# x in two halves, operand splits moved into the projections they follow, and output blocks between the last MLA scores

## The reference, cut to what matters

```python
def mla_layer(x, pos, norm_g, w_in, q_norm_g, w_q_up, kv_norm_g, w_kv_up, q_gain, k_gain, w_out):
    z = rms_norm(x, norm_g) @ w_in
    cq, ckv, k_pe, gate = jnp.split(z, [...], axis=-1)          # 512, 512, 64, 2048 wide
    q = (rms_norm(cq, q_norm_g) @ w_q_up).reshape(b, s, A_HEADS, A_QK)
    kv = (rms_norm(ckv, kv_norm_g) @ w_kv_up).reshape(b, s, A_HEADS, A_NOPE + A_V)
    ...
    o = mla_attend(q, k, v, pos).reshape(b, s, A_WIDTH)         # masked softmax(q k) v
    return x + (o * jax.nn.silu(gate)) @ w_out

def diff_layer(x, pos, layer_idx, norm_g, w_in, q_gain, k_gain, lq1, lk1, lq2, lk2, subln_g, w_out):
    z = rms_norm(x, norm_g) @ w_in                              # q, k, v, gate: each 2048 wide
    ...
    o = diff_attend(q, k, v, pos, lam)                          # softmax - lam * softmax, times v
    o = rms_norm(o, subln_g) * (1.0 - lam_init)
    return x + (o.reshape(b, s, B_WIDTH) * jax.nn.silu(gate)) @ w_out
```

## Time and profile before

| | us |
|---|---|
| median of 3 runs | 3446.47 |
| lowest, highest | 3445.31, 3449.75 |
| the profiled execution | 3445.53 |
| its span in the profile | 3443.7 |
| PE busy | 3324.7 (97%) |
| DVE busy | 1534.2 (45%) |
| POOL busy | 2101.6 (61%) |
| ACT busy | 707.8 (21%) |
| mean granted clock | 0.982 of 2.4 GHz |

### The profile page before, as it was taken

The page is one execution under the profiler, slowest core; times in us unless marked ns, Lnnn a source line. Parts: engine busy times, 40 slices in busy tenths (PEclk is TensorE's granted clock), DMA queues, the critical chain, the costliest instruction groups (busy, mean ns, idle before and its releaser), DMA issues.

```text
span 3443.7 us, 63823 instructions
## 1 busy us (share of the span) xinstructions
PE 3324.7 (97%) x21442; PEld 2648.1 (77%) x21442; DVE 1534.2 (45%) x3108; ACT 707.8 (21%) x1284; POOL 2101.6 (61%) x3492
## 2 busy tenths in 40 slices
PE   8999999998999989899989998999999999999899
PEld 6777777777787877678867777787888888788687
DVE  3444444445666763571246666213433243323500
ACT  2111111102323220130024444101211111111200
POOL 6444444445767748688764433787666666766566
PEclk9999999999999989899999999999999999999999
DMA  4111111112222213223321111232222222222232
GB/s 152 51 50 45 50 50 50 44 50 68 71 75 67 73 49 92 76 79 92 92 63 39 39 37 37 83 95 83 74 79 79 73 73 73 80 74 78 61 104 79
DMA packets 459579, 239.42 MB, mean 70 GB/s; under 512 B 27901, under 2 KB 456120, under 8 KB 458936
## 3 DMA queue, kind: packets, MB, share of 16 engines
q1 hardware_dynamic: 455656, 232.19, 23.1%
q10 hardware_dynamic: 3792, 5.28, 0.4%
HBM read 233.22 MB, written 4.19 MB: 69 GB/s over the span
## 4 chain that ended last, share of the span: by engine, by line
PE 85%; DVE 6%; issue 4%; POOL 2%; ACT 1%; SPq 1%; DVEq 0%; DMA 0%; ACTq 0%; POOLq 0%; PEldq 0%
PE proj L321 23%; PE proj L322 21%; PE proj L323 21%; POOL w_lo L311 2%; PE work L2293 2%; PE work L1114 1%; PE work L656 1%; PE work L670 1%; PE work L1926 1%; PE work L664 1%; PE work L630 1%; PE work L321 1%; PE work L639 1%; PE work L323 1%; PE work L322 1%
## 5 line engine op out<-in xcount | busy, mean ns | idle before, releaser
L307 POOL TENSOR_SCALAR w_hi<-raw_weights 128x256 fp32r<-128x256 f32 x1744 | 745.3, 455 | 1326.3 <-PE proj L323 1310.6
L311 POOL TENSOR_TENSOR w_lo<-raw_weights,w_hi 128x256 fp32r<-128x256 f32 x1744 | 1372.5, 818 | 0.0
L321 PE MATMUL proj<-x_hi,w_hi 128*128 128x512 f32 x2976 | 1234.1, 415 | 40.5 <-POOL w_lo L311 14.1
L322 PE MATMUL proj<-x_lo,w_hi 128*128 128x512 f32 x2976 | 1183.3, 398 | 0.0
L323 PE MATMUL proj<-x_hi,w_lo 128*128 128x512 f32 x2976 | 1182.8, 397 | 0.0
L321 PEld LDWEIGHTS proj<-x_hi,w_hi 128*128 128x128 f32 x2976 | 563.6, 189 | 205.5 <-issue 48.5
L323 PEld LDWEIGHTS proj<-x_hi,w_lo 128*128 128x128 f32 x2976 | 563.0, 189 | 138.0
L322 PEld LDWEIGHTS proj<-x_lo,w_hi 128*128 128x128 f32 x2976 | 565.1, 190 | 117.0 <-issue 2.2
L321 PE MATMUL proj<-o_hi,w_hi 128*128 128x512 f32 x256 | 103.5, 404 | 7.3 <-POOL w_lo L311 3.6
L321 PE MATMUL proj<-lat_hi,w_hi 128*128 128x512 f32 x224 | 97.5, 435 | 8.6 <-DVE lat_lo L1733 4.0
L322 PE MATMUL proj<-o_lo,w_hi 128*128 128x512 f32 x256 | 102.1, 399 | 0.0
(11 more groups left out here) (465 smaller groups left out, 4251.4 us busy)
## 6 DMA issues: line engine op xcount, KB each, us to landing
raw_weights<-w_in SPq DMA_DIRECT2D x260, 256.0 KB, 3.2
raw_weights<-b_w_in SPq DMA_DIRECT2D x256, 256.0 KB, 3.1
raw_weights<-a_w_in SPq DMA_DIRECT2D x100, 256.0 KB, 3.2
raw_weights<-w_out SPq DMA_DIRECT2D x64, 256.0 KB, 2.9
raw_weights<-a_w_out SPq DMA_DIRECT2D x64, 256.0 KB, 3.0
raw_weights<-b_w_out SPq DMA_DIRECT2D x64, 256.0 KB, 2.9
raw_weights<-a_w_kv_up SPq DMA_DIRECT2D x32, 256.0 KB, 2.8
mix<-x SPq DMA_DIRECT2D x4, 1024.0 KB, 8.2
```

The source lines that it names most:

```text
L307: pool.tensor_scalar(part(hi_v, s % 2, q), part(raw_v, s, q), 1.0, 1.0, ALU.mult, ALU.mult).then_inc(hi_done, 1)
L311: pool.tensor_tensor(part(lo_v, s % 2, q), part(raw_v, s, q), part(hi_v, s % 2, q).bitcast(F32), ALU.subtract).then_inc(w_split, 1)
L321: pe.matmul(out, w_h, a_h, start=start, stop=False)
L322: pe.matmul(out, w_h, a_l, start=False, stop=False)
```

## The change

Eight edits, in the order of the program.

1. `x_hi` and `x_lo` become two buffers each, for blocks 0 to 7 and 8 to 15, laid out hi0, lo0, hi1, lo1. `xh` and `xl` are now lists of blocks. PSUM banks are numbered anew (`j % 4`, `LAT_BANK`, `MLA_BANK`).
2. At the ends of LAT, MLA and OUT2 a new `stage_left` takes the place of most `stage_end` calls: it counts and does not wait.
3. LAT: the four q latents are split during the last latent tile; the sums of the kv latents stand in MLA behind 4 blocks; each kv split follows the norm of its block.
4. MLA's last pair: OUT2's first-half blocks stand where other pairs have projection blocks, four ahead of the first scores, one in each step, two in each of the last two. Operand blocks 0 to 3 are split ahead of the first scores, 4 to 7 one in each of steps 4 to 7, 8 to 15 behind the pair.
5. OUT2's last group: blocks 0 to 7 of DIFF's operand are split between its additions, once its first halves are done; blocks 8 to 15 behind it.
6. DIFF: the sums of squares stand behind its first tile, and the reciprocal root follows them.
7. DIFF's last head: the eight OUT3 splits stand ahead of the last gate (`before_scores()` moves up one line), and ACT starts them when half of the last tile is projected.
8. OUT1's loop over groups is unrolled.

```diff
+        x_parts = [[fixed.take(f"x_{part}{g}", UNIT_KB * SEQ, F32R) for part in ("hi", "lo")] for g in range(2)]
...
+        def stage_left(eng, own):
+
+            for s, value in own:
+                eng.wait_ge(s, value)
+            eng.sem_inc(stage_done, 1)
...
+                if k == 2 * LB - 2:
+                    tile_done(act, U_LAT + 4 * LB - 2)
+                    latent_high(act, range(LB))
...
             for k in range(LB, 2 * LB):
-                scaled(lat[:, k], U_LAT + 2 * k + 1, proj[BANK(T_LAT, k)])
+                if k == 2 * LB - 1:
+                    for b in range(LB):
+                        latent_low(dve, b)
+                scaled(lat[:, k], U_LAT + 2 * k + 1, proj[LAT_BANK(k)])
...
             pe.wait_ge(LN2_DVE.sem, LN2_DVE.done(f"lo{LB - 1}"))
-            run(part, 5)
+            run(part, LB)
+            sums_of_latent(pe, 1)
+            run(part, LB)
             kv_rstd_pe(pe)
-            run(part, 7)
-            pe.wait_ge(LN2_DVE.sem, LN2_DVE.done(f"lo{2 * LB - 1}"))
-            run(part, 8)
+            run(part, LB)
+            for k in range(LB, 2 * LB):
+                pe.wait_ge(LN2_DVE.sem, LN2_DVE.done(f"lo{k}"))
+                run(part, 1)
+            run(part, LB)
...
+            for parts in mla_heads_pe(pe, A_HEADS // 2 - 1, 4, ()):
+                run(part, parts)
+            run(part)
+            stage_left(pe, [])
...
+            two = [out_half(pe, OUT2, 0, j, 0) for j in range(2)]
+            for part in two * 2:
+                for _ in range(UNIT_KB // 2):
+                    next(part)
+                    yield
+            for j in (2, 3):
+                yield from out_half(pe, OUT2, 0, j, 0)
...
+                    if k >= TB:
+                        split(range(k, k + 1))
...
+                if TB <= k < HB:
+                    split(range(k, k + 1))
...
+            for j, before, between in ((0, range(0, 4), ()), (1, range(4, 6), ()), (2, range(6, 8), ()), (3, (), range(8, 9))):
+                norm_b_low(dve, before)
+                add_tile(dve, OUT2, KB // 4 - 1, j)
+                norm_b_low(dve, between)
+                add_squares(KB - 4 + j)
+            norm_b_low(dve, range(9, KB))
...
             def split_first():
-                act.wait_ge(w_used, SPLIT_SLOTS + U_OUT3)
+                tile_done(act, U_OUT3 - 2)
                 out_split_act(act, OUT3, FIRST)
...
+            before_scores()
             gate_tanh_of(1)
-            before_scores()
...
+            before_scores()
             take_gate(1)
-            before_scores()
```

More of the change, by code:

```diff
@@ L244, in build @@
         lo_v = w_lo[:, :].rearrange("p (s k c) -> p s k c", s=SPLIT_SLOTS, k=UNIT_KB)
-        xh = tokens(x_hi[:, :], SEQ)
-        xl = tokens(x_lo[:, :], SEQ)
+        xh, xl = ([tokens(x_parts[b // UNIT_KB][part][:, :], SEQ)[:, b % UNIT_KB] for b in range(KB)]
+                  for part in range(2))
         mix_v = tokens(mix[:, :], SEQ)
@@ L1037, in build @@
         o_lo4 = tokens(nc.alloc_sbuf_tensor_at("o_lo4", [P, KB * SEQ], F32R, offset=o_start)[:, :], SEQ)
-        OUT1 = OutStage("out1", 4, U_OUT1, T_OUT1, mix_v, o_hi4, o_lo4)
+        OUT1 = OutStage("out1", 4, U_OUT1, T_OUT1, mix_v, *([v[:, b] for b in range(KB)] for v in (o_hi4, o_lo4)))
         OUT1.o_hi_at = stage_start
@@ L1413, in add_tile @@
                 dve.tensor_tensor(acc_q[:, :], acc_q[:, :], q4[:, :], ALU.add).then_inc(d_summed, 1)
-            for j in range(4):
-                add_tile(0, j)
-            with dve.Fori(1, KB // 4) as i:
+            for i in range(KB // 4):
                 for j in range(4):
@@ L2026, in mla_heads_dve @@
             done(dve.tensor_tensor(m_qr[:, :], m_qr[:, :], m_tmp[:, :], ALU.add), "qrr")
+            split(range(0, 4))
             need(MA_PE, "sums")
@@ L2096, in build, with add_tile @@
         h_all_summed = sem("h_all_summed")
[L2098 to L2109 removed]
+        def add_tile(dve, st_, i, j, group=None):
+            c = 4 * i + j
+            tile_done(dve, out_last_unit(st_, i, j))
+            h = flat(mix_v[:, bass.ds(c, 1), :])
+            out = h if group is None else group[:, j]
+            dve.tensor_tensor(out, h, proj[j % 4][:, :], ALU.add).then_inc(tile_free, 1)
         def out2_pe(pe):
[L2112 removed]
             for j in range(4):
@@ L2118, in out2_pe, with square @@
                         run(out_half(pe, OUT2, i, j, h))
-            pe.wait_ge(h_summed, KB + 2)
-            token_sums(pe, work[0], sq[1], lambda b: b).then_inc(h_all_summed, 1)
-            stage_end(pe, 7, [(h_all_summed, 1)])
+            stage_left(pe, [])
         def out2_act(act):
-            out_split_act(act, OUT2, range(KB))
-            with act.Fori(0, KB) as c:
+            last_pair = A_HEADS // 2 - 1
+            for k in LAST:
+                if k >= KB - 2:
+                    act.wait_ge(MA_DVE.sem, MA_DVE.done(f"g{TB * (k - KB + 3) - 1}", last_pair))
+                out_split_act(act, OUT2, (k,))
+            def square(c):
                 act.wait_ge(tile_free, T_OUT2 + c + 1)
@@ L2379, in diff_dve @@
         def diff_dve(dve):
[L2380 to L2383 removed]
+            dve.wait_ge(h_all_summed, 1)
             token_rinv(dve, NB_DVE, work[0][:, 0:4])
@@ L2549, in out3_dve @@
             out_split_dve(dve, OUT3, LAST)
-            add_tiles(dve, OUT3, y_group, OT_PE)
+            with dve.Fori(0, KB // 4) as i:
+                dve.wait_ge(OT_PE.sem, OT_PE.after(i))
+                for j in range(4):
+                    add_tile(dve, OUT3, i, j, y_group)
             stage_end(dve, 9, [(tile_free, T_OUT3 + KB)])
```

172 lines of the change are left out of this document (92 added, 80 removed).

## The result

The changed kernel takes 3438.7 us (median of 6 runs) against 3448.11 before (6 runs): a ratio of 0.9975 with the 95% interval 0.9965 to 0.9985, faster by 9.4 us where 11 were forecast. In a second session it took 3433.92 (5 runs) against 3448.04: 0.996 (0.9946 to 0.9973). One of the six runs, 3446.8 us, has a mean granted clock of 0.935 where the other five have 0.983 to 0.986.

The account below looks back on a forecast made before the run. TensorE is busy 97% of the span, so only its remaining gaps can be won. The terms 9.2 - 8.0 + 6.0 + 4.0 = 11.2 us gave a median of 3435.5 us, range 3424 to 3447.

Parts of the forecast that it names:

- LAT to MLA: LAT's end to MLA's rotation: 20.2 us instead of 29.4, paced by GpSimd's weight splits; gain 9.2.
- that bound of 7.0: LAT's end to MLA's rotation: lower gain, with 6.15 us for both GpSimd units and a fall of the clock (22.4 us).
- the 18.2 that the prediction gives for that case: LAT's end to MLA's rotation in us if every GpSimd unit takes 4.35; gain 11.2.
- MLA's last pair: Fill blocks of OUT2 wait for their own step's splits, 6.8 us a step, and the clock falls; loss 8, bounds 1 and 11.
- I take 7 of the 9: MLA's last pair: 2.2 us a step at 1.2 GHz, 9 over the steps following a gap, of which 7 counted.
- The first rival, the clock holds: MLA's last pair: the stall chain is there but TensorE keeps 2.4 GHz; 7 us back, 3428.5; chance 0.14.
- OUT2 to DIFF: OUT2's end to DIFF's second tile, with 1.0 before it: 14.8 us for 20.8, delayed by GpSimd contention; gain 6.0.
- The bound of 7.5 without contention: OUT2's end to DIFF's second tile: upper gain, 7.5 us, if VectorE's splits don't slow GpSimd.
- DIFF's last head: OUT3's splits start earlier; second score pair at 3221.1 instead of 3225.14, one wait of 1.1 left; gain 4.0, bounds 2.5 and 5.
- No cost elsewhere: Other banks, the two halves of x and the unrolled OUT1 loop: 0, hidden under TensorE.
- GpSimd shut out: VectorE's runs of SBUF operations block GpSimd in five places; 16 us more, 3451.5, above the old time; chance 0.06.

Follow-up runs that it names:

- Experiment 7: The kernel of experiment 3, with ScalarE making the high half behind the step's exponential instead of ahead of it; 3423.2 us (one run).
- experiment 5: Changed kernel with the low-half subtractions of the latents and DIFF's operand replaced by memsets of zero; 3431.3 us (one run).
- experiment 4: Changed kernel with twelve needless matmuls ahead of each of the four waits in steps 4 to 7 of MLA's last pair; 3432.1 us (one run).
- experiment 3: Changed kernel with operand blocks 4 to 7 split one step ahead of their fill block, high half ahead of the exponential; 3419.34 us, 0.9915 of before.
- experiment 2: Changed kernel with MLA's last pair and OUT2's splits put back as before the change; 3430.47 us, 0.9946 of before.
- Experiment 6: Changed kernel with OUT3's eight splits still ahead of the last gate, but started only when the last tile is projected; 3441.1 us (one run).
- experiment 1: The changed kernel once more, unaltered, in a second session; 3433.92 us, 14.1 below before.

## Why the prediction was right or wrong

The sum was right, 11.2 forecast, 9.4 and 14.1 measured in two sessions, and the stretches of the first profile add to -6.8 + 4.9 + 2.1 - 7.0 - 3.9 = -10.7 (-10.5 with the fourth score set for the third). It is that near by luck: two of the four terms were too large by 2.4 and 3.1 us, with opposite signs, and the larger of them changes from execution to execution.

- **LAT to MLA: 9.2 forecast, 6.8 measured.** GpSimd as the pace was right, with two waits of 2.3 and 2.1 (2 to 3 forecast), and the third unit ended 12.9 behind LAT's end, as worked out (13.0). Mis-sized: the fourth unit, taken at 4.35, met the kv splits too and took 5.16; and eight matmuls at 1.2 GHz followed the waits, which stood only in the bound. The unit has 0.8 of the 2.4 us, the matmuls about 1.6 (eight at 0.43 from start to start instead of 0.23). The measured gain lies just beyond that bound of 7.0. Experiment 7, where the clock's fall was hidden, has 20.9 us (20.2 and the unit's 0.8), and experiment 5, with every unit at 4.35, has the 18.2 that the prediction gives for that case.
- **MLA's last pair: a loss of 8 forecast, 4.9 and 1.8 measured.** The mechanism was right: four waits of 3.35 for x_lo (3.5 forecast), a step of 6.8 at the full clock. In experiment 4, where the clock holds, the stretch is 0.6 longer than before, and 0.9 was worked out. The term that failed is "I take 7 of the 9" for the clock. It cost 4.3 us in the first profile and 1.4 in the second (8.13 and 6.82 against 6.80). A slow step can cost more than the 2.2 taken for it (2.8 for step 4 of the first profile), but not all four waits were followed by one. That the stall was in the order of the splits and not in the fill is shown by experiment 3; that the excess over 6.8 is the clock, by experiment 4. The first rival, the clock holds, is nearer to the second session than the forecast was.
- **OUT2 to DIFF: 6.0 forecast, 7.0 - 2.1 = 4.9 measured.** The wait behind OUT2's end was 1.71 for 1.4. The splits under OUT2's last tiles cost 0.9 + 0.1 + 0.5 + 0.1 = 1.6 in the four units where 1.0 was taken, and another 0.6 came from the operand splits of blocks 8 to 15, now under OUT2's fourth unit, which the forecast gave no price (in experiment 2, with those splits back in their place, it is gone and the rest of OUT2 is 158.4). Experiment 5 shows that the units' excess and nearly all of the wait are GpSimd's. The bound of 7.5 without contention doesn't follow from the terms beside it: without the 1.0 and the 1.4 they give 12.4 for 20.8, a gain of 8.4, and experiment 5 has 9.0 less the 0.6 above.
- **DIFF's last head: 4.0 forecast, 3.9 measured** (3.7 by the fourth score set, which is the one at 3225.14 that the forecast priced), with the one wait (1.04 for 1.1). Experiment 6 shows that it is the early start and not the order, which by itself loses.
- **No cost elsewhere** was right: experiment 1 reaches LAT's end as before does.
- **GpSimd shut out** was a rival and did not come: no wait for w_lo in the first profile exceeds 2.8 us, and where the change is, none exceeds 2.3 (experiment 1 has one of 3.7, within the first 25 us of the kernel). In each place it had begun its set ahead of VectorE's run, or stood in it already, and they took turns. The Trainium skill ("SBUF — State Buffer", Who interferes with whom) says that the shared pair is an exclusive lock, that whoever issues first has it for the whole instruction (said of VectorE's 2-port modes), and that an instruction of VectorE with two SBUF inputs contends with one of GpSimd that reads SBUF. This case's trace agrees in the order: in the set of 4.58 each w_lo instruction lasts 1.17 to 1.18 instead of 0.74, and VectorE's between them 1.21 to 1.23 instead of 0.69, one of each in turn. Each is longer by 0.4 to 0.5, less than an instruction of the other lasts alone, so the trace doesn't show the pair held over the whole of a recorded instruction. The extension to whole runs of VectorE instructions was mine, from the one case in the earlier trace rows.

What stays open: why equal waits of 3.35 us were followed by slow matmuls once, twice or three times in different executions; experiment 5, with the same four waits, had distances of 8.42, 9.41 and 8.21.

## What to carry to other kernels

Where work is put between the steps of a chain as fill, its own operands must be ready one step before: here one step and the place of one ScalarE copy turned a loss of 2 to 5 us into a gain of 14. A low-part subtraction on VectorE, with two inputs in SBUF, cost GpSimd 0.43 to 0.46 us each here (a w_lo instruction 1.17 instead of 0.74, a w_hi one 0.84 to 0.87 instead of 0.41), so it has to be counted against the slack of GpSimd's unit and not against VectorE's own. And a small change is better judged by stretches between the same matmuls of two profiles than by the total: one wait far from the change, and the lower clock behind it, moved the first profile by 5 us.

## What the runs showed of the hardware

- The granted clock behind equal waits isn't repeatable: four waits of 3.35 us cost 4.3, 1.4 and 1.5 us (experiment 6: distances of 8.24, 6.82, 6.81) in three executions of the same instructions, and 5.6 in experiment 5.
- Needless matmuls in the waits kept 2.4 GHz in all four (experiment 4: 0.55 us of each wait was left idle, and no matmul of the stretch lasted 0.63).
- VectorE's two-input instructions and GpSimd's weight splits took turns, one of each: 1.17 instead of 0.74 for a w_lo instruction and 1.22 instead of 0.69 for a low half.
- Ten profiles reach LAT's end, with no relevant difference ahead of it, at 1751.6 (two), 1753.3 to 1755.3 (six) and 1758.8 to 1759.0 (two). The last two have a wait of 2.28 and 2.83 us in RWKV that is put down to instruction issue, and the lower clock behind it, 5.3 and 6.0 us together.
